# The entry of a two-layer decoder kernel on one Trainium2 core: gate products, scaled inputs and key products in another order

## The reference

```python
for i in range(2):                       # layer 0: forgetting attention, layer 1: latent attention
    shift, scale, gate = ada_modulation(c, ada_w[i, 0], ada_b[i, 0])   # silu(c) @ w + b, split in three
    h = rms_norm(x) * (1.0 + scale) + shift
    y = forgetting_attention(h, ...) if i == 0 else latent_attention(h, ...)
    x = x + gate * y
    shift, scale, gate = ada_modulation(c, ada_w[i, 1], ada_b[i, 1])
    h = rms_norm(x) * (1.0 + scale) + shift
    x = x + gate * conv_gated_mlp(h, ...)
return rms_norm(x) * final_g
# forgetting_attention: q, k, v, f = split(h @ w_in); cum = cumsum(log_sigmoid(f + b_f));
# scores = q k^T / 8 + cum_q - cum_k, causal softmax, times v, @ w_o
```

## Time and profile before

| what | us |
|---|---|
| median of 3 runs | 1274.04 (1274.01 to 1274.13) |
| the profiled execution | 1274.12 |
| its span, from the first to the last instruction | 1271.8 |
| TensorE busy in it | 1244.1 (98%) |
| VectorE busy | 852.0 (67%) |
| ScalarE busy | 547.4 (43%) |

### The profile page before, as it was taken

How to read it: one execution, slowest core, us unless ns; L and a number is a source line. 1 busy time by engine, 2 the same in 40 slices (tenths; PEclk the granted TensorE clock), 3 DMA queues, 4 the chain that set the end, 5 groups by cost and what they waited for, 6 DMA issues and landing times.

```text
span 1271.8 us, 17575 instructions
## 1 busy us (share of the span) xinstructions
PE 1244.1 (98%) x6393; PEld 983.8 (77%) x6393; DVE 852.0 (67%) x1283; ACT 547.4 (43%) x1003; POOL 39.5 (3%) x45
## 2 busy tenths in 40 slices
PE   6999999999999999999999999999999999999997
PEld 4677777777888878788888766668788888888886
DVE  3766676658988888855447777756876666663332
ACT  6644454545433333322235566654633333332222
POOL 2000000003000000000020000001100000000000
PEclk9999999999999999999999999999999999999999
DMA  9633543342656666566533222122233333333332
GB/s 319 195 88 95 166 129 92 129 116 71 200 182 188 190 193 193 158 190 196 165 96 83 47 34 34 38 67 83 83 100 89 93 98 99 99 95 92 91 93 94
DMA packets 248494, 154.69 MB, mean 122 GB/s; under 512 B 52729, under 2 KB 236510, under 8 KB 245354
## 3 DMA queue, kind: packets, MB, share of 16 engines
q1 hardware_dynamic: 248426, 153.76, 41.0%
HBM read 151.60 MB, written 2.14 MB: 121 GB/s over the span
## 4 chain that ended last, share of the span: by engine, by line
PE 86%; DVE 7%; ACT 5%; issue 2%; DMA 0%; SPq 0%; DVEq 0%; ACTq 0%
PE pj L1889 73%; PE ov L2195 3%; PE tr L2170 2%; DVE wl L1278 2%; PE sc L2143 1%; ACT wh L808 1%; PE sc L2425 1%; ACT soft L989 1%; DVE tmp L1389 1%; PE pj L2391 1%; PE sc L2157 1%; PE ov L2425 1%; DVE xT L1566 1%; ACT tmp L982 0%; DVE hl L1377 0%
## 5 line engine op out<-in xcount | busy, mean ns | idle before, releaser
L1278 DVE TENSOR_TENSOR wl<-raw,wh 128x1024 fp32r<-128x1024 f32 (+2 forms) x196 | 228.5, 1166 | 241.1 <-ACT wh L808 239.0
L808 ACT ACTIVATE wh<-raw 128x1024 fp32r<-128x1024 f32 (+2 forms) x196 | 195.6, 998 | 432.7 <-PE pj L1889 424.3
L1889 PE MATMUL pj<-hh,wh 128*128 128x512 f32 x912 | 361.4, 396 | 4.8 <-DVE wl L1278 4.7
L1889 PE MATMUL pj<-hh,wl 128*128 128x512 f32 x912 | 356.7, 391 | 0.0
L1889 PE MATMUL pj<-hl,wh 128*128 128x512 f32 x912 | 355.2, 389 | 0.0
L1889 PE MATMUL pj<-gh,wh 128*128 128x512 f32 x560 | 222.9, 398 | 4.0 <-DVE gl L1407 2.2
L1889 PE MATMUL pj<-gh,wl 128*128 128x512 f32 x560 | 218.8, 391 | 0.0
L1889 PE MATMUL pj<-gl,wh 128*128 128x512 f32 x560 | 218.6, 390 | 0.0
L1889 PEld LDWEIGHTS pj<-hh,wh 128*128 128x128 f32 x912 | 171.3, 188 | 44.3 <-ACT gh L1195 4.9
L1889 PEld LDWEIGHTS pj<-hh,wl 128*128 128x128 f32 x912 | 171.2, 188 | 36.0
L1889 PEld LDWEIGHTS pj<-hl,wh 128*128 128x128 f32 x912 | 171.5, 188 | 33.2
(11 more groups left out here) (287 smaller groups left out, 1277.4 us busy)
## 6 DMA issues: line engine op xcount, KB each, us to landing
raw<-in_ffn_w_in_dram SPq DMA_DIRECT2D x88, 512.0 KB, 3.8
ada_w_sb<-in_ada_w_dram SPq DMA_DIRECT2D x40, 1024.0 KB, 5.2
raw<-in_ffn_w_out_dram SPq DMA_DIRECT2D x32, 448.0 KB, 3.7
raw<-in_fox_w_in_dram SPq DMA_DIRECT2D x22, 512.0 KB, 3.9
raw<-in_ffn_w_out_dram SPq DMA_DIRECT2D x16, 512.0 KB, 4.0
raw<-in_fox_w_o_dram SPq DMA_DIRECT2D x8, 512.0 KB, 4.0
raw<-in_mla_w_o_dram SPq DMA_DIRECT2D x8, 512.0 KB, 4.0
raw<-in_mla_w_a_dram SPq DMA_DIRECT2D x5, 512.0 KB, 3.9
```

Source lines behind the costliest of these rows:

```text
L808: act.activation(wh[:, n0 % 2, 0:kt, :], (raw_tile(n0) if not per else raw[:, n0 % 2, :, :])[:, 0:kt, :], ACT.Copy).then_inc(w_hi, 1)
L1278: dve.tensor_tensor(wl[:, n0 % 2, 0:kt, :], (raw_tile(n0) if not per else raw[:, n0 % 2, :, :])[:, 0:kt, :], f32(wh[:, n0 % 2, 0:kt, :]), ...
L1889: ins = pe.matmul(bank_[:, :], (low if term == 2 else high)[:, kt, :], (rl if term == 1 else rh)(kt), start=start and j == 0, stop=stop an ...
```

## The change

TensorE's list of the entry gets another order: the gate products 0 to 3 stand in two pairs around query products 2 and 3, key products 0 to 3 move up to the third block, key products 4 to 7 to the fifth block, and `f_shift_sum` follows them. Six of the eight constants products go, and `turn_block(0)` stands ahead of `spread(0)`. All copies into `xT` go to VectorE. On ScalarE, the weight split `C_FOX + 2` goes ahead of `high`, of which three stand ahead of Abs, Exp and Ln and five behind them; the copy of `cum` goes ahead of the table load for Exp and of the weight split `C_FOX + 3`. On VectorE, `h_lows(1 to 7)` and `z_scaled(0)` go behind the gate's bias. The eighth scaled input gets room of its own in `ada_w_sb`, so that `ada_load(1)` and what follows on SP's list now wait for all `h`. The gate and key weights are loaded one block earlier.

```diff
         def first_pre(kt):
+            if kt == DT - 1:
+                return ada_w_sb[:, 1, S:2 * S]
             return (mid if kt < 4 else soft)[:, (8 + kt % 4) * S:(9 + kt % 4) * S]
...
# SP
-                if b == 2:
+                if b == 1:
                     sp.dma_start(f_raw[:, :, :], fox[:, 3 * D:3 * D + HEADS].rearrange("(t p) n -> p t n", p=P)
                                  ).then_inc(f_in, 16)
                     first_weight(1)
...
             sp.wait_ge(f_shift, 1)
+            sp.wait_ge(h_hi, DT)
+            sp.wait_ge(h_lo, DT)
             ada_load(1)
...
# ACT
-                act.wait_ge(x_t, 2 * t + 1)
-                act.activation(xT[:, 0:4, t * P:(t + 1) * P], SC[0][:, :], ACT.Copy).then_inc(x_e, 1)
...
             block_take(1)
+            act.wait_ge(f_in, 16)
+            act.activation(f_wh[:, :, :], f_raw[:, :, :], ACT.Copy).then_inc(f_hi, 1)
             act.wait_ge(block_ok, 2)
             first_high(2)
             first_high(3)
+            split(C_FOX + 1)
             act.activation(early[:, 7:8], eps[:, 0:1], ACT.Exp)
-            act.wait_ge(f_in, 16)
-            act.activation(f_wh[:, :, :], f_raw[:, :, :], ACT.Copy).then_inc(f_hi, 1)
             block_take(2)
-            split(C_FOX + 1)
...
             first_z(0)
-            act.wait_ge(block_ok, 4)
-            for kt in range(4):
-                high(0, kt)
             block_take(4)
             split(C_FOX + 2)
+            act.wait_ge(block_ok, 4)
+            for kt in range(3):
+                high(0, kt)
             act.wait_ge(block_ok, 5)
-            for kt in range(4, DT):
-                if kt == DT - 2:
-                    act.wait_ge(f_bias_s, 1)
-                    act.wait_ge(fg_d, 1)
-                    act.activation(fga[2], fga[0], ACT.Abs, bias=f_bias[:, 0:1]).then_inc(fg_a, 1)
-                high(0, kt)
+            act.wait_ge(f_bias_s, 1)
+            act.wait_ge(fg_d, 1)
+            act.activation(fga[2], fga[0], ACT.Abs, bias=f_bias[:, 0:1]).then_inc(fg_a, 1)
...
             act.activation(fga[4], fga[3], ACT.Ln, bias=ones[0:HEADS, 0:1]).then_inc(fg_a, 1)
+            for kt in range(3, DT):
+                high(0, kt)
             act.wait_ge(qk_row, 1)
...
+            act.wait_ge(fg_d, 5)
+            act.activation(cum[HD:HD + 3 * HEADS, :], cum[0:3 * HEADS, :].bitcast(F32), ACT.Copy).then_inc(cum_ok, 1)
             act.activation(early[:, 7:8], eps[:, 0:1], ACT.Exp)
             split(C_FOX + 3)
-            act.wait_ge(fg_d, 5)
-            act.activation(cum[HD:HD + 3 * HEADS, :], cum[0:3 * HEADS, :].bitcast(F32), ACT.Copy).then_inc(cum_ok, 1)
...
# DVE
             for t in range(QB):
-                dve.wait_ge(x_t, 2 * t + 2)
-                dve.tensor_copy(xT[:, 4:DT, t * P:(t + 1) * P], SC[1][:, :].rearrange("p (k q) -> p k q", q=P)
-                                ).then_inc(x_ev, 1)
+                for f in range(2):
+                    dve.wait_ge(x_t, 2 * t + f + 1)
+                    dve.tensor_copy(xT[:, 4 * f:4 * f + 4, t * P:(t + 1) * P], SC[f][:, :].rearrange("p (k q) -> p k q", q=P)
+                                    ).then_inc(x_e, 1)
...
+            first_pres((DT - 1,))
+            block_mod(4)
+            dve.wait_ge(block_ok, 4)
+            split(C_FOX + 2)
+            h_lows((0,))
             dve.wait_ge(f_mm, 1)
             dve.wait_ge(rb_copy, 1)
             dve.tensor_tensor(fga[0], F_PSUM[0:HEADS, :], rb_sb[0:HEADS, :], ALU.mult).then_inc(fg_d, 1)
-            first_pres((DT - 1,))
-            dve.wait_ge(block_ok, 4)
-            h_lows(range(4))
-            split(C_FOX + 2)
-            block_mod(4)
...
             dve.tensor_scalar(fga[1], fga[0], f_bias[:, 0:1], 0.0, ALU.add, ALU.min).then_inc(fg_d, 1)
-            h_lows(range(4, DT))
+            h_lows(range(1, DT))
+            z_scaled(0)
...
# PE
-            constants_products(1)
             block_rows(0)
-            spread(0)
             pe.wait_ge(pick_ok, 2)
             turn_block(0)
-            constants_products(4)
+            spread(0)
+            constants_products(2)
             first_product(0, 0)
             block_rows(1)
             first_product(0, 1)
             turn_block(1)
-            constants_products(3)
+            f_product(0)
+            f_product(1)
             first_product(0, 2)
             first_product(0, 3)
+            f_product(2)
+            f_product(3)
             block_rows(2)
-            f_product(0)
+            first_product(1, 0)
             turn_block(2)
             for kt in range(1, 4):
-                f_product(kt)
+                first_product(1, kt)
...
-            first_product(1, 0)
             block_rows(4)
-            first_product(1, 1)
-            first_product(1, 2)
+            first_product(1, 4)
             turn_block(4)
-            first_product(1, 3)
+            first_product(1, 5)
+            first_product(1, 6)
+            first_product(1, 7)
             f_shift_sum()
-            for kt in range(4, DT):
-                first_product(1, kt)
...
-                if kt == 1:
+                if kt == 5:
                     pe.wait_ge(qk_row_sb, 1)
```

More of the change, by code:

```diff
@@ L418, in build @@
         rb_copy = sem("rb_copy")
-        x_ev = sem("x_ev")
         block_ok = sem("block_ok")
@@ L882, in _ @@
                 act.activation(squares, xs[t], ACT.Square, accum_out=x_ssq[:, t:t + 1]).then_inc(sq, 1)
-                act.wait_ge(x_t, 2 * t + 1)
-                act.activation(xT[:, 0:4, t * P:(t + 1) * P], SC[0][:, :], ACT.Copy).then_inc(x_e, 1)
             act.wait_ge(sq, QB)
             act.activation(stat[:, 0, :], x_ssq[:, :], ACT.Sqrt, bias=eps[:, 0:1], scale=1.0 / D).then_inc(dev, 1)
-            act.wait_ge(x_e, QB)
-            act.wait_ge(x_ev, QB)
+            act.wait_ge(x_e, 2 * QB)
             block_take(0)
@@ L1438, in _ @@
             norm(0)
-            dve.wait_ge(x_e, QB)
-            dve.wait_ge(x_ev, QB)
+            dve.wait_ge(x_e, 2 * QB)
             block_mod(0)
@@ L1445, in _ @@
             block_mod(1)
+            dve.wait_ge(f_hi, 1)
+            dve.tensor_tensor(f_wl[:, :, :], f_raw[:, :, :], f32(f_wh[:, :, :]), ALU.subtract).then_inc(f_lo, 1)
             dve.wait_ge(block_ok, 2)
             first_lows((2, 3))
+            split(C_FOX + 1)
             dve.wait_ge(rb, 1)
-            first_pres((0, 1))
-            dve.wait_ge(f_hi, 1)
-            dve.tensor_tensor(f_wl[:, :, :], f_raw[:, :, :], f32(f_wh[:, :, :]), ALU.subtract).then_inc(f_lo, 1)
+            first_pres(range(4))
             block_mod(2)
-            split(C_FOX + 1)
             dve.wait_ge(block_ok, 3)
             first_lows(range(4, DT))
-            first_pres(range(2, DT - 1))
+            first_pres(range(4, DT - 1))
             block_mod(3)
-            z_scaled(0)
+            first_pres((DT - 1,))
[3 more added lines that the diff above has]
+            h_lows((0,))
             dve.wait_ge(f_mm, 1)
@@ L2000, in _ @@
                     if t:
-                        pe.wait_ge(x_ev if f else x_e, t)
+                        pe.wait_ge(x_e, 2 * t + f - 1)
                     for q in range(4):
@@ L2077, in _ @@
             pe.wait_ge(sil, 1)
-            pe.wait_ge(x_e, QB)
-            pe.wait_ge(x_ev, QB)
+            pe.wait_ge(x_e, 2 * QB)
             pe.wait_ge(pc, 11)
-            constants_products(1)
             block_rows(0)
-            spread(0)
             pe.wait_ge(pick_ok, 2)
             turn_block(0)
-            constants_products(4)
+            spread(0)
+            constants_products(2)
             first_product(0, 0)
```

## The result

The changed kernel takes 1278.71 us (median of 6 runs, 1278.07 to 1279.5) against 1274.09 for the kernel before (6 runs, 1273.94 to 1274.91): ratio 1.0036, 95% interval 1.0024 to 1.0048, so 4.6 us slower. That is the forecast's direction and inside its range, but above the own range of the likeliest case (1276.3 to 1278.3) and at the sum of the clock rival, 1278.9. The profiled execution took 1278.07, the fastest of the six, with a span of 1275.8 against 1271.8 before: 4.0 us more in the span. One execution of the kernel of experiment 12 took 1550.4 us at a mean granted clock of 0.751, where all others here have 0.992 or more; it is left out of that experiment's numbers.

What follows compares the result with a forecast made beforehand. TensorE's list was taken to bound the kernel almost everywhere. 2.8 us won up to `f_shift_sum` against 6.2 us of new waits behind it gave +3.4 on 1274.1: 1277.5 us, range 1275.8 to 1279.5.

Steps and rivals of the forecast that it cites:

- the likeliest case: Whole kernel: new waits behind the gate chain outweigh the front's gain, clock stays up; 1277.5 us, 1276.3 to 1278.3, chance 0.55.
- the clock rival: TensorE's clock falls in the new waits, first `C_FOX + 3` matmuls run at half speed: 1.4 us more, 1278.9, chance 0.20.
- The front: Entry up to `f_shift_sum`: fewer waits and constants put the new order 2.8 us ahead there.
- T: Start of the first gate-block product: 14.4 us instead of 15.78, so 1.4 us won, between 0.8 and 2.8.
- A: Start of the first query product: 4.63 us after the first gate-block product starts, as before, so at 19.0 us.
- F: Start of `f_shift_sum`: 28.4 us after the first query product starts, so at 47.4 us.
- The chain behind F: From `f_shift_sum` through Ln, five `high`, low parts, running sum, `cum` and weight split to `C_FOX + 3`: 16.15 us.
- The waits: TensorE between `f_shift_sum` and `C_FOX + 3`: three new waits of 2.1, 2.6 and 1.5 us, together 6.2 us.
- The sum: Start of `C_FOX + 3`: 63.55 instead of 60.16 us, +3.4, from 2.8 us won and 6.2 us of new waits.
- not told apart: Rival at the front: first gate-block product starts by 13.5 us, change stays within 0.2%; 1276.1 at the bound, chance 0.18.
- TensorE's own work alone: Rival behind `f_shift_sum`: the wait for the gate chain stays hidden, 2.8 us remain won; 1271.3, chance 0.07.
- Costed at nothing: Eighth input's own room, earlier split of `C_FOX + 2` and later transfers cost nothing; `C_FOX + 4` covered by 1.7 us.

Runs made afterwards that it cites:

- experiment 12: Experiment 9's kernel with the eighth scaled input in its old room and its transfers early again: 1271.28 us, ratio 0.9975 to the kernel before.
- Experiment 10: Experiment 9's kernel with the copies of x shared by ScalarE and VectorE as before: 1272.1 us, ratio 0.9982 to the kernel before.
- after_again: Experiment 1: the changed kernel run again without edit: 1279.0 us, ratio 1.0037 to the kernel before.
- fill_third_wait: Experiment 2: the changed kernel with eleven constants products in TensorE's wait ahead of the scores: 1276.76 us, ratio 1.0022 to the kernel before.
- experiment 6: The kernel before with only the new ScalarE and VectorE order behind the third block, and the query and key shift's turn moved: 1279.6 us, ratio 1.0042.
- experiment 9: The changed kernel's front with another order behind: all `high` ahead of Abs, low parts around the bias, weight split before `cum`: 1270.52 us, ratio 0.9972.
- experiment 2: The changed kernel with eleven constants products in TensorE's wait ahead of the scores: 1276.76 us, ratio 1.0022 to the kernel before.
- experiment 7: The changed kernel with ScalarE's and VectorE's lists behind the third block put back as before: 1275.07 us, ratio 1.0009 to the kernel before.
- experiment 3: The changed kernel with Exp table load and split of `C_FOX + 3` ahead of `cum`: 1276.33 us, ratio 1.0016 to the kernel before.
- experiment 4: The changed kernel with the early table load and split, plus eleven constants products ahead of the scores: 1275.37 us, ratio 1.0012 to the kernel before.
- experiment 5: The changed kernel with all eight `high` ahead of Abs, Exp and Ln on ScalarE: 1277.0 us, ratio 1.0023 to the kernel before.

## Why the prediction was right, and where its sum was off

**The front: right, its gain a little too small.** T is 14.18 (forecast 14.4), A follows 4.47 later (4.63), F 27.95 after that (28.4): F is 46.60, and the front is 3.6 instead of 2.8 us ahead. The gate product's wait for its own weight is 0.45 against the 0.6 that was estimated; the rest is spread over small terms. Experiment 10 shows T's share at the end.

**The chain behind F: right.** Ln ends at F + 4.33 (forecast F + 4.25), the last low part at F + 8.37 (8.3), `cum` at F + 11.73 (11.75), the scores start at F + 13.3 (13.2), `C_FOX + 3` at F + 16.25 (16.15). The waits are 2.06 and 2.71 for 2.1 and 2.6. The third is 0.32 instead of 1.5, because the scores ran at the lower clock and ended later; where they did not, it is 1.43 (after_again) and 1.42 (fill_third_wait). Experiments 6 and 9 show that this chain is the order's doing: alone it costs 5.6 us (3.7 of later start, the rest the clock), without it the front's gain arrives.

On the table loads the row was the right choice: in the changed kernel Ln begins at 50.21, where the load has ended at 48.91 + 1.28 = 50.19, and the small Exp likewise at 60.30 behind 60.29. The Trainium skill ("ScalarE: Activation LUTs", section "What ACT_TABLE_LOAD costs") adds a drain to each switch; no such gap shows in these rows.

**The sum:** +3.4 was forecast for the start of the product, and +2.7 measured (+2.4 and +2.5 in experiments 1 and 2). The difference is the larger gain at F.

**The clock: the step that failed.** "I expect the delay to stay to the end" with a clock at 1.00 was the likeliest case, and the falling clock a rival at 0.20. The fall shows in both profiled executions of the changed kernel, the mean clocks point to it in the others too, and experiment 2 gives its price: 2.2 us on average, where the rival took 1.4. It is added to the forecast's chain and does not replace it. The time lies inside the range because the range reached to this rival; the likeliest case's own sum, 1277.5, is 1.2 us short. And that the rival's total, 1278.9, was nearly met is in part luck: two errors nearly cancelled, the chain 0.7 to 1.0 too dear, the clock 0.8 too cheap. What the case against the rival leaned on, dense work before the first wait, did not prevent it.

**The other rivals.** T was never 13.5 or less in a profile here, so "not told apart" did not arise. "TensorE's own work alone" was wrong for this order, and its two conditions were the right ones: experiment 9 meets both (no `high` behind Ln, no low part that holds the sum) and lands at 1270.5 where the rival's sum was 1271.3. They are not enough by themselves: what the rival left out is the place of ScalarE's table load and split, which ahead of `cum` hold the scores in experiment 7, and behind it the product in the changed kernel.

**Costed at nothing: held.** No wait for a transfer shows in the changed kernel around the second product, and experiment 12 finds no measurable worth in the moved transfers, in the reordered kernel.

## What to carry to other kernels

When work is taken out from under a chain of small dependent steps, walk that chain through the lists of all engines that carry it: what stands between two of its links (here five `high` with their low parts, and a weight split) is its delay. Reordering those lists turned 4.6 us of loss into 3.5 us of gain with the same work. Count a wait of TensorE like those here twice: once as the wait, and once as the slower matmuls behind it, since the clock fell in or right behind waits of 1.43 to 2.77 us (the changed kernel, experiments 1 and 3 to 7), though not at each of them. To price the second alone, fill the wait with matmuls that nobody reads.

## What the runs showed of the hardware that was not expected

The granted clock fell at a different moment in each execution: in the second wait in the changed kernel (0.72 from 58 to 60), in the third in its second profile (0.91 from 60 to 62), and once already right behind the first (experiment 4). The price went from 1.3 to 2.8 us with it. So kernels near such a fall scatter more: experiments 3 and 4 spread over 2.4 and 2.3 us, the changed kernel over 1.4, experiments 2 and 9, whose profiles show no fall in the entry, over 0.6.

A lower mean clock was not a longer time. Of the eleven executions of the changed kernel, the five at 0.994 took 1277.99 to 1278.83 us, the five at 0.996 took 1278.81 to 1279.5. The two profiles suggest why: the early fall spends part of its slow stretch in the waits, where it costs nothing, the late one most of it in the dense product. With one profile of each this is argued, not shown.

T itself differed by 0.5 us (13.86 and 14.34) between kernels whose work up to there is the same: in the second, the transposes of the later blocks ran slowly for longer (16 in 3.38 us, against 8 in 1.42 and 8 in 1.19). Why is not shown: the clock column reads 1.00 there in both.
